# Stick-breaking attention weights: logarithms and triangular sums on TensorE, or two sigmoids, a multiplying scan and transposes

## The reference

```python
def stick_breaking_attention(q, k, v):
    """A[t,s] = beta_ts * prod_{s<j<t} (1 - beta_tj), s < t only."""
    ...
        z = jnp.einsum('bqhd,bshd->bhqs', qb, kb).astype(jnp.float32) * scale
        ...
        strict = s_idx < t_idx
        log_keep = jnp.where(strict, -jax.nn.softplus(z), 0.0)
        tail = lax.cumsum(log_keep, axis=3, reverse=True) - log_keep
        w = jnp.where(strict, jnp.exp(jax.nn.log_sigmoid(z) + tail), 0.0)
        outs.append(jnp.einsum('bhqs,bshd->bqhd', w.astype(v.dtype), vb))
```

## Time and profile before

| what | value |
|---|---|
| time, median of 3 runs | 2773.27 us (2772.57 to 2779.37) |
| span of the profiled execution | 2770.7 us |
| PE busy | 2717.8 us (98%) |
| DVE busy | 1515.3 us (55%) |
| ACT busy | 1160.4 us (42%) |
| granted clock of PE | 9 (full) in each of the 40 slices |
| one pair of the first layer, from its value transposes to the next pair's | 58.35 us |

### The profile page before, as it was taken

One profiled execution on the slowest core, in us unless ns is written; L12 is line 12 of the kernel. 1 busy time (PEld: TensorE's weight loads), 2 busy tenths in 40 slices (PEclk: granted clock), 3 DMA queues, 4 the chain that ended last, 5 costly groups with the idle time before them and its releaser, 6 DMA issues.

```text
span 2770.7 us, 30662 instructions
## 1 busy us (share of the span) xinstructions
PE 2717.8 (98%) x12366; PEld 2189.4 (79%) x12366; DVE 1515.3 (55%) x2093; ACT 1160.4 (42%) x1734; POOL 114.2 (4%) x79
## 2 busy tenths in 40 slices
PE   8999999999999999999999999999999999999998
PEld 6888878888887888887666888888876668888887
DVE  5666657465787747477444454444554445544443
ACT  6444344243475424254545333322444553333322
POOL 2333110000010000000000000000000000000000
PEclk9999999999999999999999999999999999999999
DMA  4111113223322322222111222222221112222222
GB/s 171 53 58 58 50 59 106 94 91 107 107 99 91 111 93 99 99 99 91 46 38 47 91 98 93 99 98 92 99 77 38 46 46 99 92 99 96 99 94 76
DMA packets 66955, 235.64 MB, mean 85 GB/s; under 512 B 7552, under 2 KB 8320, under 8 KB 66816
## 3 DMA queue, kind: packets, MB, share of 16 engines
q1 hardware_dynamic: 63504, 228.58, 23.7%
q10 hardware_dynamic: 3312, 5.12, 0.6%
HBM read 231.57 MB, written 2.10 MB: 84 GB/s over the span
## 4 chain that ended last, share of the span: by engine, by line
PE 86%; ACT 6%; DVE 5%; issue 2%; POOL 1%; DMA 0%; SPq 0%; ACTq 0%; DVEq 0%
PE bank L412 25%; PE bank L414 25%; PE bank L413 25%; PE bank L766 1%; PE bank L827 1%; ACT w_hi_k L897 1%; PE bank L755 1%; PE bank L806 1%; PE bank L746 1%; DVE w_lo_k L1393 1%; PE bank L758 1%; POOL q_mix L2003 1%; PE bank L819 1%; PE bank L562 0%; DVE xr_lru L1691 0%
## 5 line engine op out<-in xcount | busy, mean ns | idle before, releaser
L412 PE MATMUL bank<-x_hi_k,w_hi_k 128*128 128x512 f32 x2152 | 873.8, 406 | 11.8 <-DVE x_lo_k L1400 10.9
L897 ACT ACTIVATE w_hi_k<-raw_k 128x1024 fp32r<-128x1024 f32 x431 | 454.4, 1058 | 962.4 <-PE bank L414 960.3
L414 PE MATMUL bank<-x_hi_k,w_lo_k 128*128 128x512 f32 x2152 | 842.5, 391 | 0.0
L413 PE MATMUL bank<-x_lo_k,w_hi_k 128*128 128x512 f32 x2152 | 841.1, 391 | 0.0
L1393 DVE TENSOR_TENSOR w_lo_k<-raw_k,w_hi_k 128x1024 fp32r<-128x1024 f32 x431 | 532.8, 1236 | 174.4 <-ACT w_hi_k L897 174.4
L412 PEld LDWEIGHTS bank<-x_hi_k,w_hi_k 128*128 128x128 f32 x2152 | 406.0, 189 | 110.2 <-issue 14.1
L414 PEld LDWEIGHTS bank<-x_hi_k,w_lo_k 128*128 128x128 f32 x2152 | 405.2, 188 | 86.2
L413 PEld LDWEIGHTS bank<-x_lo_k,w_hi_k 128*128 128x128 f32 x2152 | 406.3, 189 | 84.2 <-issue 4.1
L412 PE MATMUL bank<-y_hi_k,w_hi_k 128*128 128x512 f32 x1136 | 445.5, 392 | 4.5 <-DVE y_lo_k L1726 3.2
L414 PE MATMUL bank<-y_hi_k,w_lo_k 128*128 128x512 f32 x1136 | 442.7, 390 | 0.0
L413 PE MATMUL bank<-y_lo_k,w_hi_k 128*128 128x512 f32 x1136 | 442.6, 390 | 0.0
(11 more groups left out here) (316 smaller groups left out, 2516.4 us busy)
## 6 DMA issues: line engine op xcount, KB each, us to landing
raw_k<-wstream SPq DMA_DIRECT2D x431, 512.0 KB, 3.2
outT<-h_k ACTq DMA_DIRECT2D x8, 256.0 KB, 2.9
h_k<-xT SPq DMA_DIRECT2D x4, 256.0 KB, 8.4
h_k<-xT ACTq DMA_DIRECT2D x4, 256.0 KB, 7.8
decay_mix<-constants ACTq DMA_DIRECT2D x4, 256.0 KB, 2.6
levels_mix<-constants SPq DMA_DIRECT2D x1, 448.0 KB, 11.3
vec_k<-vectors SPq DMA_DIRECT2D x1, 282.5 KB, 10.0
cos_mix<-constants SPq DMA_DIRECT2D x1, 256.0 KB, 10.3
```

The costliest lines, as they stand in the source:

```text
L412: pe.matmul(dst, wh, rh, start=start, stop=False)
L413: pe.matmul(dst, wh, rl, start=False, stop=False)
L414: return pe.matmul(dst, wl, rh, start=False, stop=stop)
L897: act.activation(k.w_hi[:, u % SPLIT, :], k.raw[:, u % RAW, :], ACT.Copy).then_inc(*hi_done.mark())
```

## The change

The stick-breaking weights are computed with queries on partitions and keys along the row. For each head the four query tiles i are taken from the last to the first, with 512, 384, 256 and 128 keys seen (`seen_keys`). PE's logits have the roles of queries and keys exchanged. ACT computes sigmoid(-z) into `keep` and sigmoid(z) into `stick_w`. DVE runs a multiplying scan over `keep` along the keys, from the last key to the first (both views are reversed), into `kept`, and multiplies `stick_w` with it, shifted by one key. PE turns the weights in 128 x 128 pieces (function `turned`), ACT copies them out of the bank (`stick_wT`), and PE multiplies each piece with the values (`output`, one 128-column product for each query tile and key tile seen). The sigmoids need another table set than Ln and Exp, so table loads stand around the window's Ln and Exp. The stick task has 23 steps in place of 21, spread over the first 0.92 of the pair.

```diff
-STICK_STEPS = 1 + 2 * (2 * TC + 1) + 1 + 1
+STICK_STEPS = 1 + 2 * (2 * TC + 2) + 1 + 1
...
-    return ((stick, STICK_STEPS, 0, 1), (window, WINDOW_STEPS, 0, 0.95),
+    return ((stick, STICK_STEPS, 0, 0.92), (window, WINDOW_STEPS, 0, 0.95),
...
-        def log_weights(n, half, s):
...
-            mm = pe.matmul(z_view(k, s), k.negs[:, 0, :], keys_view(k.sp_t, s), ...
-            if s < TC - 1:
-                mm = pe.matmul(z_view(k, s)[:, P:], k.negs[:, 1, :], keys_view(k.sp_t, s + 1), ...
...
+        def turned(n, i):
+            pe.wait_ge(*dve_done.at("stick_w", *at, n))
+            pe.wait_ge(*(act_done.at("stick_wT", *at, n - 1) if n > 0 else act_done.at("vt", *at)))
+            for s in range(i + 1):
+                mm = pe.transpose(ch(bank[4], s), ch(k.stick_w[:, n % 2], s), k.ident)
...
+        def output(n, half, i):
...
+            pe.wait_ge(*act_done.at("stick_wT", *at, n))
+            for s in range(i + 1):
+                mm = pe.matmul(bank[5][r, i * P:i * P + P], k.vt[:, s, r], ch(k.stick_wT[:, n % 2], s), ...
...
+            if n >= 2:
+                output(n - 2, *STICK_ORDER[n - 2])
+            if 1 <= n <= 2 * TC:
+                turned(n - 1, STICK_ORDER[n - 1][1])
...
-                act.activation(e, z_view(k, j), ACT.Abs).then_inc(*mark())
...
-                act.activation(e, e, ACT.Exp, scale=-1.0).then_inc(*mark())
...
-                act.activation(e, e, ACT.Ln, bias=1.0).then_inc(*mark("e", *at, n))
...
+                act.activation(k.keep[:, n % 2, 0:seen_keys(i)], z, ACT.Sigmoid, scale=-1.0).then_inc(*mark())
+                act.activation(k.stick_w[:, n % 2, 0:seen_keys(i)], z, ACT.Sigmoid)...
...
+                act.activation(k.stick_wT[:, (n - 1) % 2, 0:seen_keys(i)], bank[4][:, 0:seen_keys(i)], ACT.Copy)...
...
+        ln_exp_tables()
         act.wait_ge(*pe_done.at("wq_sum", *at))
         inverse_root(k.rstd[:], bank[6][:], 1.0 / 64, "wq_root", *at)
+        sigmoid_tables()
...
+            ln_exp_tables()
             act.wait_ge(*dve_done.at("max", *at, half))
...
+            if half == 0:
+                sigmoid_tables()
...
+                dve.tensor_tensor_scan(k.kept[:, T - seen_keys(i):T][:, ::-1], keep[:, ::-1],
+                                       k.zeros[:, 0:1].to_broadcast([P, seen_keys(i)]), 1.0, ALU.mult,
+                                       ALU.add).then_inc(*mark())
+                dve.wait_ge(*now())
+                dve.tensor_tensor(w, w, k.kept[:, T - seen_keys(i) + 1:T + 1], ALU.mult)...
```

More of the change, by code:

```diff
@@ L303, in attention_memory @@
     k.st = take("st", [P, 5, TC])
-    k.zk, k.zwk = take("zk", [P, 2, T]), take("zwk", [P, 2, T])
     arena.at = shared
@@ L307, in attention_memory @@
     k.m_hi, k.m_lo = take("m_hi", [P, KT, T], F32R), take("m_lo", [P, KT, T], F32R)
+    k.zk, k.zwk = take("zk", [P, 2, T]), take("zwk", [P, 2, T])
     arena.at = shared
@@ L351, in interleave @@
         assert next(steps, None) is None
-STICK_STEPS = 1 + 2 * (2 * TC + 1) + 1 + 1
+STICK_STEPS = 1 + 2 * (2 * TC + 2) + 1 + 1
 WINDOW_STEPS = 6 + 2 * 9 + 1
-STICK_ORDER = [(half, j) for half in range(2) for j in reversed(range(TC))]
-Z_BANK_OF = {2: 0, 4: 2, 5: 1, 6: 4, 7: 3}
+STICK_ORDER = [(half, i) for half in range(2) for i in reversed(range(TC))]
 def filling(fill, parts):
@@ L734, in stick, with logits @@
         if pair > 0:
-            pe.wait_ge(*act_done.at("att_o", layer, pair - 1))
+            pe.wait_ge(*act_done.at("stick_wT", layer, pair - 1, 2 * TC - 1))
         for c in range(TC):
-            mm = pe.transpose(ch(bank[5], c), ch(k.lands[2], c), k.ident)
+            mm = pe.transpose(ch(bank[4], c), ch(k.lands[2], c), k.ident)
         mm.then_inc(*mark("v_t", *at))
         yield
-        def logits(n, half, j):
+        def logits(n, half, i):
             if n == 0:
                 pe.wait_ge(*dve_done.at("qk", *at))
-            if n in Z_BANK_OF:
-                pe.wait_ge(*act_done.at("weights", *at, Z_BANK_OF[n]))
-            pe.matmul(z_view(k, j), k.zk[:, half, j * P:j * P + P], k.aq[:, j * P:T], start=True, stop=False)
-            pe.matmul(z_view(k, j)[:, 0:P], k.id_b[:], k.mask_b[:, 0:P], start=False,
-                      stop=True).then_inc(*mark("z", *at, n))
@@ L762, in output @@
-        def output(half):
-            r = slice(half * 64, half * 64 + 64)
-            pe.wait_ge(*act_done.at("weights", *at, half * TC + TC - 1))
-            for s in range(TC):
-                mm = pe.matmul(bank[5][r, s * P:T], k.vt[:, s, r], keys_view(k.w_t, s), start=s == 0,
-                               stop=s == TC - 1)
-            return mm
-        for n in range(2 * TC + 1):
+            if n >= 2:
+                pe.wait_ge(*act_done.at("stick_keep", *at, n - 2))
+            z = z_view(k, n, i)
@@ new lines, in output @@
+        def output(n, half, i):
+            r = slice(half * 64, half * 64 + 64)
+            if n == 0 and pair > 0:
+                pe.wait_ge(*dve_done.at("att_y", layer, pair - 1))
+            pe.wait_ge(*act_done.at("stick_wT", *at, n))
+            for s in range(i + 1):
+                mm = pe.matmul(bank[5][r, i * P:i * P + P], k.vt[:, s, r], ch(k.stick_wT[:, n % 2], s), start=s == 0,
+                               stop=s == i)
+            mm.then_inc(*mark("att_o", *at, n))
+        for n in range(2 * TC + 2):
@@ L1254, in stick @@
         act.wait_ge(*pe_done.at("v_t", *at))
-        act.activation(k.vt[:], by_tile(bank[5]), ACT.Copy).then_inc(*mark("vt", *at))
+        act.activation(k.vt[:], by_tile(bank[4]), ACT.Copy).then_inc(*mark("vt", *at))
         yield
-        for n in range(2 * TC + 1):
+        for n in range(2 * TC + 2):
             if n < 2 * TC:
-                half, j = STICK_ORDER[n]
-                e = k.e_t[:, n % 2, 0:T - j * P]
+                half, i = STICK_ORDER[n]
                 act.wait_ge(*pe_done.at("z", *at, n))
@@ L1262, in stick @@
                 if n >= 2:
-                    act.wait_ge(*dve_done.at("softplus", *at, n - 2))
-                act.activation(e, z_view(k, j), ACT.Abs).then_inc(*mark())
-                act.wait_ge(*now())
-                act.activation(e, e, ACT.Exp, scale=-1.0).then_inc(*mark())
-                act.wait_ge(*now())
-                act.activation(e, e, ACT.Ln, bias=1.0).then_inc(*mark("e", *at, n))
-            yield
-            if n:
-                half, s = STICK_ORDER[n - 1]
-                act.wait_ge(*pe_done.at("log_w", *at, n - 1))
-                act.activation(keys_view(k.w_t, s), z_view(k, s),
-                               ACT.Exp).then_inc(*mark("weights", *at, n - 1))
+                    act.wait_ge(*pe_done.at("stick_wT", *at, n - 2))
@@ L1275, in stick @@
             yield
-        act.wait_ge(*pe_done.at("att_o", *at))
-        act.activation(k.ao[:], bank[5][:], ACT.Copy).then_inc(*mark("att_o", *at))
+        act.wait_ge(*pe_done.at("att_o", *at, 2 * TC - 1))
+        act.activation(k.y_hi[:, pair, :], bank[5][:], ACT.Copy).then_inc(*mark("att_y", layer, pair))
         yield
-        act.wait_ge(*now())
-        act.activation(k.y_hi[:, pair, :], k.ao[:], ACT.Copy).then_inc(*mark("att_y", layer, pair))
         if pair < 3:
```

82 lines of the change are left out of this document (38 added, 44 removed).

## The result

| | before | after |
|---|---|---|
| median, us | 2773.36 (2772.57 to 2779.37) | 2791.3 (2789.56 to 2791.92) |
| profiled execution, span us | 2770.7 | 2789.9 |
| mean granted clock of PE | 0.998 | 0.995 |
| the four pairs of layer 1, us | 58.80, 58.35, 58.33, 59.97 | 59.29, 61.64, 61.60, 61.50 |
| the four pairs of layer 2, us | 58.80, 58.36, 59.98, 58.36 | 59.31, 61.60, 61.59, 61.63 |

What follows compares the result with a forecast made beforehand. PE was taken to bound the kernel nearly everywhere, with one ACT and DVE chain beating it in a pair. Waits of +5.0 us against -4.8 us of PE work for most pairs summed to 0.0: 2773 us, range 2757 to 2789.

Steps and rivals of the forecast that it cites:

- The chains: ACT and DVE work PE waits for in a pair: four waits, 7.7 us in place of 2.7.
- First transposes, scores, third output: PE's waits in a pair ahead of weight transposes, window scores and third output: 3.05, 2.65 and 1.4 us.
- The fourth wait: PE's wait for the second half's probabilities in a pair: 0.6 us.
- the sum: Waits +5.0 against PE work -4.8, +0.2 us for six pairs; -0.6 us for two first pairs; total 0.0.
- 20 output products of 128 columns, 20 x 0.22 = 4.4: PE work added in each pair by the new stick-breaking outputs: 4.4 us, at 0.22 us a product.
- my 4.5: PE work removed in each pair with the two old outputs: 4.5 us taken, from 4.6, or 4.3 by columns.
- a full clock: PE's granted clock was read as full in every slice of the page before the change.
- A granted clock that falls behind the longer waits: Listed sign that the forecast is wrong: PE's clock falling behind the longer waits; no size or chance given.
- the places in memory: Moved places in memory, taken as far from what PE waits for; uncovered, with other small edits, some tenths of a us.
- The gain stays: Rival: ACT's loads cost its queue nothing, 3.9 us less for each pair, 2742 (2742 to 2765); chance 0.25.
- The slower scan: Rival: DVE's scan over reversed views takes 2.45 us for 512, first wait grows 1.2 us a pair, 2783; chance 0.13.
- the costlier switch: Rival: each ACT table-set switch costs the load's 1.3 us a second time, 4.6 x 8 = 37 us, 2810; chance 0.08.

Runs made afterwards that it cites:

- run with few loads: Changed kernel with query tiles smallest first, stick task over 0.97 of the pair, parts from its start, table loads only where the set changes: 2739.43 us.
- the spare products in both kernels: Spare bf16 matmuls where PE waits: changed kernel, 12 before first weight transposes, 10 before scores, 2784.0 us; kernel before, 10 before scores, 2770.25 us.
- the run with wide weights: Changed kernel with output products using all 128 columns of a value tile as weights instead of 64, written into all 128 rows: 2776.84 us.
- the run with one set of tables: Changed kernel with the window's Ln and Exp replaced by Sigmoid and none of the 40 table loads: 2762.63 us.
- the rewoven kernel: Changed kernel without a pair's first table load, stick task spread over the whole pair, parts begun at 0.05 instead of 0.1: 2771.89 us.

## Why the prediction was wrong, point by point

- *The chains held.* First transposes, scores, third output: 3.06, 2.44 and 1.17 shown, against 2.9, 2.5 and 1.3 forecast. The fourth wait came as 0.18 where 0.6 was worked out (0.45 as shown). All waits of the attention together grew from 20.6 to 51.9 us; with the 0.15 that the trace shows too little for each of three more waits in eight pairs that is +34.9, against 38.4 in the sum (6 x 5.0 + 2 x 4.2).
- *The step that failed: "20 output products of 128 columns, 20 x 0.22 = 4.4".* It was sized by products with 128-column weights, though the code shows `k.vt[:, s, r]` with 64. In the pair they take 20 x 0.22 + 8 x (0.14 + 0.10) = 6.3 us. Part of that comes off again: the two old outputs had such edges too (2.30 + 0.10 us each, so 0.3 more than my 4.5). So by count PE's own work falls by 4.8 - 1.9 + 0.3 = 3.2 us, not 4.8. The run with few loads measures it: 54.50 less its wait of 1.94 (from the issue of L747 at 1361.79 to 1363.76) is 52.56, against the 55.65 of before, 3.1 less. Over eight pairs the mis-sized term is 1.7 x 8 = 13.6 us, the larger part of the 18.
- *The second: a full clock, taken for granted.* "A granted clock that falls behind the longer waits" stood only in the list of what would show the forecast wrong, without a price and without a chance. A 9 on the page is "90% or more", not "full", as I read it, and its slices of 69 us were too coarse to show before's two falls; windows of 10 us show both. They follow the very wait that I took apart, 2.5 us ahead of the scores, and the change puts one of 3.06 us ahead of it. Price: six falls in place of two at 1.6 to 1.65 us, 6.6 us (8.6 us of lost work, not all of which is time).
- *A third, small: the places in memory, "some tenths of a us".* In each layer the 192 products that read `m_hi` and `m_lo` take 0.8 us more altogether (44.56 us from the first to the last in layer 1, 43.73 before), and from `merge` to the next layer's first pair every variant of the changed kernel takes 516.7 us, every variant of before 515.9. These tiles, and what lies beside them, moved in memory; no run tells whether that is the reason. Over two layers this is 1.6 us.
- *The sum again.* PE's work -3.1 x 8 = -24.8; waits +34.9; together +10.1 (the pairs without falls say 6 x 1.6 + 2 x 0.5 = 10.6). Clock +6.6; the products on `m_hi` and `m_lo` +1.6: +18.3. Measured: +19.2 in the profiled spans. 0.9 us are left over, some 0.6 of them behind the last product.
- *The rivals.* The gain stays: false, the loads stood in the chain as argued. The slower scan and the costlier switch: false by the rows above. What happened was none of the three: the run was slower on PE's own side, by its clock and its narrow weights.
- *What carries which proof.* That a fall costs 1.6 us of a pair, and so 9.9 us of the changed kernel and 3.2 of before, is shown by the spare products in both kernels; the loads put into before point the same way. That the output groups are dear by 0.24 us, 15 us in all, is shown by the prices from start to start in the run with wide weights; its whole time also moved through waits and clock, and is no proof by itself. Why PE needs 0.10 and 0.14 us at such an edge is open: no run here tells it.

## What to carry to other kernels

When a chain beside TensorE is lengthened, price the clock with the wait: look for its falls in windows of about 10 us, not on the page, and see what length of wait stands ahead of those that are there. A load of function tables costs its 1.3 us where it stands in the chain that TensorE waits for; count the loads at each point, those included that repeat the set in place. And take a product's price from a row whose weights are as wide as its own, with its neighbours on both sides.

## What was not expected of the hardware

- TensorE's clock falls to its lower level for some 3.4 us (6.8 in one pair of after) behind waits of 2.3 to 3.1 us in a stretch that is otherwise busy, at 1.7 us of lost work a time; one such wait in a pair is enough (the run with one set of tables), and not each one is followed by a fall (before: two falls behind eight waits of up to 2.54). In the pairs of the run with few loads, with waits of up to 1.75 us, there was none. But the length of the wait doesn't decide alone: in the first block a wait of 1.85 us ends at 859.64 us in that same run with the clock falling (0.83 in 860 to 870), and before has the same wait at 858.79 without a fall.
- A group of f32 matmuls with 64-column weights between groups of 128-column ones costs 0.24 us more than its columns: 0.10 ahead (0.33 against 0.23) and 0.14 behind (0.36, 0.80 and 1.02 for 2, 6 and 8 matmuls against 0.22, 0.66 and 0.89 with 128 columns).
- A load of the table set that is already in place takes the full 1.28 us (14 us in the whole kernel, clock included), and where the sigmoid's set is in place and no load is asked for, Ln and Exp each get one of their own (6 and 6 in the rewoven kernel).
- The multiplying scan takes 1.23 us over 512 elements, reversed or not the earlier trace rows.
